# Expert weights in 2 MB transfers, with each expert's units in the order gate, gate, up, up, down, down

## The chip, the core and the metric

The kernel runs on one core of a Trainium2 chip. The metric is the time in microseconds of one execution on the device. Three executions of the kernel before took 1879.18, 1884.72 and 1877.73 us; their median, 1879.18 us, is what the changed kernel is compared with.

The engines are named as in the profile: PE multiplies matrices, and PEld is its loading of weights; DVE does elementwise work, ACT activation functions and copies, POOL indices and gathers, and SP issues most of the DMAs. Engines run on their own and wait for each other on semaphores.

## What is computed

The program is one step of a small two-layer decoder. Layer 0 ends in a dense SwiGLU. Layer 1 ends in a mixture of eight experts, of which each token uses two:

```python
def swiglu(x, w_gu, w_down):
    F = w_down.shape[-2]
    gu = x @ w_gu
    return (jax.nn.silu(gu[..., :F]) * gu[..., F:]) @ w_down

def moe_swiglu(x, w_router, w_gu, w_down):
    logits = jnp.einsum('btd,de->bte', x, w_router).astype(jnp.float32)
    top_val, top_idx = lax.top_k(logits, TOP_K)
    gates = jax.nn.softmax(top_val, axis=-1)
    ...
    for e in range(N_EXP):
        y = y + combine[..., e:e + 1] * swiglu(x, w_gu[e], w_down[e])
    return y
```

There are 264 tokens of width 1024; each expert has `w_gu` of 1024 x 7168 (gate columns first, then up columns) and `w_down` of 3584 x 1024, all in float32. The change concerns the experts alone.

## The kernel before

**Units.** An expert's weights are 42 units of 1 MB (128 partitions x 2048 numbers). The 3584 hidden columns are cut into NG = 7 groups `c` of 512. A group has two gate units and two up units (the upper and the lower 512 rows of `w_gu`, 512 columns) and two down units (256 rows of `w_down`). `ORDER` (L243, made by `unit_order`, L230) is the order of the units in a group: gate 0, up 0, gate 1, up 1, and then the two down units of group c-1. So the first group of an expert has four units, the next six have six, and two down units end the expert.

**The path of a unit.** SP fetches it into one of six buffers of 1 MB (`halves`, by `EXPERT_HALVES`), one DMA a unit (`load_unit`, the DMA is on L556). ACT copies it, rounded, into the first half of one of three split buffers (`unit_hi`, L982), and DVE writes the rounding error into the second half (`unit_lo`, a subtraction on L1091). PE then does 12 matmuls of 512 columns for it: four blocks of rows, three products of high and low parts each (`three`, L1654). In this text "hi" and "lo" are those two halves of a split.

**What waits for what.** SP waits to fetch unit u until unit u-6 has been split by DVE (semaphore `unit_split`). ACT waits for the landing of the unit and until PE has used unit u-3 (`units_used`), so at most three units stand split. PE waits for `unit_split`.

**Other work in a group.** After the second gate unit ACT computes the silu (L1040) before it splits the unit three places later; DVE multiplies it with the up product ("the hidden product", the multiplication on `sb` that L1091 shows) after the second up unit. After the next group's gate 1, PE transposes the hidden product (L1651); ACT and DVE split that (L1012 and L1091 on `split_he`) for the down units. These steps stand in each engine's program at fixed places of `ORDER`, three units behind PE.

**Between experts.** ACT scales the expert's rows (L1030); POOL adds them to a table in DRAM with an indirect DMA (L765, the scatter) and then gathers the rows of a later expert with another (L746, the gather). These use the same 16 DMA engines as the weights. ACT reloads its function table before the first split of an expert and again before its first silu.

The expert loop runs seven times, and the eighth expert is written out behind it. Of the first expert, six units are fetched early, during the mixer of layer 1.

Of the kernel before, what the change touches and what calls it, by code (L numbers as in the profile page):

```python
# [27 lines left out]
P = 128  # L28
D = 1024
KT = D // P  # L30
# [19 lines left out]
FF = 3584  # L50
FC = 512
NG = FF // FC
NE = 8
# [7 lines left out]
HALVES = 2 * SLOTS  # L61
UNITS = 6 * NG
SPLITS = 3
# [177 lines left out]


ORDER = unit_order()  # L243

LN_PARTS = {(0, 0): 0, (0, 1): KT // 2, "v": KT, (1, 0): KT + GB // 2}

# [5 lines left out]
def hybrid_step(nc, a, out):  # L252
# [4 lines left out]
    with ExitStack() as ctx:  # L257
# [270 lines left out]
        @block.sync  # L528
        def _(sp):
            def mixer_slabs(lay):  # L530
                for what, (n, slot, count, before) in slab_of.items():
                    if what[1] != lay:
                        continue
                    if before is not None:
                        sp.wait_ge(slabs_used, before + 1)
                    elif lay:

                        sp.wait_ge(sig("unit_split"), UNITS - HALVES + 2 * [1, 2, 0].index(slot) + 2)
                    src, k, cols = w_in_source(what)
                    sp.dma_start(as_slab(ring[slot], k, cols), src).then_inc(landed[slot], 16)  # L540

            def last_use(lay, slot):
                return max(n for what, (n, sl, _, _) in slab_of.items() if what[1] == lay and sl == slot) + 1

            def load_unit(u, w_gu, w_down, half, by_rows):

                kind, c, i = ORDER[u]
                w, c0, rows, cols = (w_down, 0, FC, D) if kind == "down" else (w_gu, c * FC + (FF if kind == "up" else 0), D, FC)
                if kind == "down":
                    w = w[c * FC:(c + 1) * FC]  # L550
                if by_rows:
                    w = w[i * rows // 2:(i + 1) * rows // 2, c0:c0 + cols]
                else:
                    w = w[:, c0 + i * cols // 2:c0 + (i + 1) * cols // 2]
                k = UNIT // (cols if by_rows else cols // 2)
                sp.dma_start(as_slab(halves[half], k, UNIT // k), w.rearrange("(k p) n -> p k n", p=P)).then_inc(half_landed[half], 16)  # L556

            sp.dma_start(xrows[:, 0:TT, :], a["x_prompt"][0].rearrange("(t p) d -> p t d", p=P)).then_inc(sig("x_landed"), 16)
            sp.dma_start(xrows[0:NS, TT, :], a["x_sample"].rearrange("b t d -> (b t) d")).then_inc(sig("x_landed"), 16)
            sp.dma_start(memrows[0], a["mem_prompt"][0].rearrange("(t p) d -> p t d", p=P)).then_inc(sig("mem0_landed"), 16)  # L560
            mixer_slabs(0)
            for u in range(UNITS):
                half = DENSE_HALVES[u % HALVES]
                if u >= HALVES:
                    sp.wait_ge(sig("unit_split"), u - HALVES + 1)
                else:
                    sp.wait_ge(slabs_used, last_use(0, half // 2))
                load_unit(u, a["ffn_w_gu"][0], a["ffn_w_down"][0], half, False)
            mixer_slabs(1)

            def expert_unit(e, t, u):
                if t is not None:

                    sp.wait_ge(sig("unit_split"), t * UNITS + (UNITS + u - HALVES + 1))
                load_unit(u, a["moe_w_gu"][0][bass.ds(e, 1)][0], a["moe_w_down"][0][bass.ds(e, 1)][0], EXPERT_HALVES[u % HALVES], True)


            for u in range(HALVES):
                sp.wait_ge(slabs_used, last_use(1, EXPERT_HALVES[u] // 2))
                expert_unit(0, None, u)  # L580
            with sp.Fori(0, NE - 1) as e:
                for u in range(HALVES, UNITS):
                    expert_unit(e, e, u)
                for u in range(HALVES):
                    expert_unit(e + 1, e + 1, u)
            for u in range(HALVES, UNITS):
                expert_unit(NE - 1, NE - 1, u)

            sp.wait_ge(sig("y_scattered"), 16 * NE)
            for tt in range(3):  # L590
                n = P if tt < TT else NS
                sp.dma_start(acc[0:n, tt, :], acc_dram[tt * P:tt * P + n, :]).then_inc(sig(f"acc{tt}_landed"), 16)
            sp.wait_ge(sig("routed"), 1)
            runs = sp.value_load(turn[0:1, 2 * NE:2 * NE + 1], min_val=NE, max_val=3 * NE)
            with sp.If(runs > NE):
                for chunk in (1, 2):
                    with sp.Fori(0, NE) as e:
                        n_tok = sp.value_load(counts[0:1, bass.ds(e, 1)], min_val=0, max_val=NT)
                        t = sp.value_load(turn[0:1, bass.ds(e + (chunk - 1) * NE, 1)], min_val=NE, max_val=3 * NE)
                        with sp.If(n_tok > chunk * P):  # L600
                            for u in range(UNITS):
                                expert_unit(e, t, u)
            sp.wait_ge(sig("y_out"), 16 * 3)

            for s in range(DEPTH):
                sp.wait_ge(sig(f"cache_out{s}"), 32)
            sp.wait_ge(sig("state_out"), 16)
            sp.wait_ge(sig("pstate_out"), 16)
            sp.wait_ge(sig("conv_out"), 48)
            sp.wait_ge(sig("sgu_out"), 16)  # L610
# [161 lines left out]
        def _(act):  # L772
# [203 lines left out]
            def unit_hi(t, u):  # L976

                if t is not None:
                    act.wait_ge(sig("units_used"), t * UNITS + (UNITS + u - SPLITS + 1))
                half = EXPERT_HALVES[u % HALVES]  # L980
                act.wait_ge(half_landed[half], (0 if t is None else t * 16 * NG) + 16 * (NG + u // HALVES + 1))
                act.activation(split_w[:, u % SPLITS, 0, :], halves[half], ACT.Copy).then_inc(sig("unit_hi"), 1)  # L982

            act.wait_ge(sig("attn1_lent_back"), 1)
# [47 lines left out]
            def expert(t, following):  # L1032

                for u in range(SPLITS, UNITS):
                    kind, c, i = ORDER[u - SPLITS]
                    if (kind, i) == ("gate", 1):
                        act.wait_ge(sig("units_used"), t * UNITS + (UNITS + u - SPLITS + 1))

                        act.wait_ge(sig("h_ready"), t * NG + (c - 2 + NG + 1))
                        act.activation(hsil[:, c % 2, :], ps[:, c % 2, :], ACT.Silu).then_inc(sig("silu_ready"), 1)  # L1040
                        if c:
                            hidden_T(t, c - 1)
                    if u == UNITS - 1:
                        if following:
                            gathered_hi(t + 1)
                        hidden_T(t, NG - 1)
                    unit_hi(t, u)
# [39 lines left out]
        def _(dve):  # L1087
# [479 lines left out]

            def expert(t, following, direct):
                for u in range(SPLITS, UNITS):
                    kind, c, i = ORDER[u - SPLITS]  # L1570
                    if (kind, i) == ("gate", 1) and c:
                        hidden_T(t, c - 1)
                    if (kind, i) == ("up", 1):
                        dve.wait_ge(sig("silu_ready"), t * NG + (c + 1))
                        dve.wait_ge(sig("units_used"), t * UNITS + (UNITS + u - SPLITS + 1))

                        if c >= 2:
                            dve.wait_ge(sig("T_done"), t * NG + (c - 1))
                        tt_(hgu[:, c % 2, :], hsil[:, c % 2, :], ps[:, 2 + c % 2, :], ALU.mult).then_inc(sig("h_ready"), 1)
                    if u == UNITS - 1:  # L1580
                        if following:
                            gathered_lo(t + 1)
                        hidden_T(t, NG - 1)
                    unit_lo(t, u)
                    if u == 4 and not direct:
                        selection_T(t)
# [52 lines left out]
        def _(pe):  # L1639
# [510 lines left out]
            def expert(t, following, direct):  # L2150

                pe.wait_ge(sig("xe_split"), t * 2 + 2)
                for u, (kind, c, i) in enumerate(ORDER):
                    if not direct:
                        if u == 2:
                            selection_T(t)
                        if u == 4:

                            pe.wait_ge(sig("selT_ready"), t * 2 + 2)
                            pe.wait_ge(sig("summed"), t * 3 + 4)  # L2160
                        if u == ORDER.index(("down", 0, 0)):

                            pe.wait_ge(sig("summed"), t * 3 + 6)
                    elif u == ORDER.index(("down", 0, 0)):

                        pe.wait_ge(sig("y_evicted"), t + 1)
                    if (kind, c, i) == ("down", NG - 2, 0) and following:
# [74 lines left out]
```

## Time and profile before

| | |
|---|---|
| median of three runs | 1879.18 us (1877.73 to 1884.72) |
| the profiled execution | 1885.63 us, its span 1883.9 us |
| PE busy | 1750.4 us, 93% of the span |
| DVE busy | 1239.7 us, 66% |
| ACT busy | 966.4 us, 51% |
| bytes read from HBM | 451.88 MB |
| the expert stage | from about 895 us to 1854 us |

The shares are means over unlike stages. Over the expert stage alone PE is busy nearly all the time and the DMA engines are too, so the stage has to be read by itself: what each engine waited for there, how long a fetch takes from issue to landing, and how much time lies between a landing and the use. PE's ends are modelled, and a busy PE is not proof of PE at its peak.

### The profile page before, as it was taken

The page shows a single profiled execution, that of the slowest core. Times are in us where ns is not written, and L with a number is a line of the kernel's source. Part 1 is how long each engine was busy: PE and PEld are TensorE (multiplying, and loading weights), DVE is VectorE, ACT ScalarE, POOL GpSimd, SP SyncE. Part 2 cuts the span into 40 slices and gives each one's busy share as a digit, 9 for nine tenths or more (in the row PEclk, how much of TensorE's full clock was granted, in tenths as well). Part 3 has the DMA queues.
Part 4 walks back from the last instruction along what each step waited for, and adds up shares of the span by engine and source line. Part 5 has one row for each costly group of instructions (what it writes and reads, how often), then busy time and mean ns, then how long its engine had stood idle before and what let it go on. Part 6 is the DMA issues. An engine that isn't in the chain of part 4 may idle for free.

```text
span 1883.9 us, 23515 instructions
## 1 busy us (share of the span) xinstructions
PE 1750.4 (93%) x8930; PEld 1470.7 (78%) x8931; DVE 1239.7 (66%) x1127; ACT 966.4 (51%) x846; POOL 124.8 (7%) x115
## 2 busy tenths in 40 slices
PE   7999799669999989796999999999999999999993
PEld 6867778559999958676887887888878888788882
DVE  2461345445666512235788888888888888888885
ACT  1342012143333222303777777787777777877772
POOL 4000152000000000002000001000010000000000
PEclk8997688889999989776999999999999999999997
DMA  7533002145555335015899999999999999999992
GB/s 261 197 134 103 1 0 68 35 158 189 181 183 182 135 129 176 7 47 201 286 372 360 395 377 364 383 365 394 371 369 382 363 388 380 364 385 366 381 381 75
DMA packets 212565, 465.55 MB, mean 247 GB/s; under 512 B 7368, under 2 KB 38243, under 8 KB 212451
## 3 DMA queue, kind: packets, MB, share of 16 engines
q1 hardware_dynamic: 203792, 433.20, 63.2%
q0 software_dynamic: 7568, 28.09, 5.1%
q10 hardware_dynamic: 1134, 3.29, 0.5%
q8 instruction: 47, 0.77, 0.2%
q14 instruction: 24, 0.20, 0.0%
HBM read 451.88 MB, written 12.82 MB: 247 GB/s over the span
## 4 chain that ended last, share of the span: by engine, by line
PE 73%; DVE 4%; ACT 3%; issue 1%; DMA 0%; ACTq 0%; DVEq 0%
PE ps L1654 70%; PE ps L1651 2%; DVE sb L1091 1%; DVE split_w L1091 1%; ACT split_w L982 1%; DVE sb L1337 1%; ACT sb L926 0%; PE ps L1802 0%; ACT L982 0%; ACT sb L1030 0%; DMA acc_rows<-sb,idx_to 0%; DVE sb L1362 0%; DVE sb L1624 0%; ACT sb L850 0%; DMA sb<-acc_rows 0%
## 5 line engine op out<-in xcount | busy, mean ns | idle before, releaser
L1091 DVE TENSOR_TENSOR split_w<-half_slots,split_w 128x2048 fp32r<-128x2048 f32 x378 | 860.7, 2289 | 208.3 <-ACT split_w L982 127.6
L982 ACT ACTIVATE split_w<-half_slots 128x2048 fp32r<-128x2048 f32 x336 | 643.4, 1919 | 222.1 <-PE ps L1654 169.7
L1654 PE MATMUL ps<-split_w,split_xe 128*128 128x512 f32 x2688 | 637.5, 393 | 4.6 <-DVE split_w L1091 2.9
L1654 PEld LDWEIGHTS ps<-split_w,split_xe 128*128 128x128 f32 x2688 | 500.4, 188 | 114.8 <-DVE split_w L1091 10.4
L1654 PE MATMUL ps<-sb 128*128 128x264 f32 (+11 forms) x2180 | 470.3, 378 | 51.3 <-DVEq L1339 10.5
L1654 PEld LDWEIGHTS ps<-sb 128*128 128x128 f32 (+4 forms) x2180 | 382.0, 220 | 136.7 <-issue 52.6
L1654 PE MATMUL ps<-split_w,split_he 128*128 128x512 f32 x1344 | 317.7, 391 | 0.0
L1654 PEld LDWEIGHTS ps<-split_w,split_he 128*128 128x128 f32 x1344 | 250.6, 188 | 54.4 <-issue 2.9
L1654 PE MATMUL ps<-x_hi,split_w 128*128 128x264 f32 x896 | 164.9, 286 | 13.4 <-DVE split_w L1091 13.4
L1654 PEld LDWEIGHTS ps<-x_hi,split_w 128*128 128x128 f32 x896 | 140.2, 191 | 13.8 <-DVE split_w L1091 13.8
L949 ACT ACTIVATE split_w<-half_slots 128x2048 fp32r<-128x2048 f32 x42 | 80.2, 1913 | 94.0 <-PE ps L1654 94.0
L1654 PE MATMUL ps<-x_lo,split_w 128*128 128x264 f32 x448 | 127.8, 285 | 0.0
L1091 DVE TENSOR_TENSOR sb<-sb,ps 128x384 f32<-128x384 f32 (+2 forms) x172 | 94.4, 567 | 46.0 <-PE ps L1654 41.7
L1651 PE MATMUL ps<-sb 128*128 128x128 f32 (+5 forms) x590 | 93.1, 299 | 30.4 <-DVEq L1191 7.0
L1651 PEld LDWEIGHTS ps<-sb 128*128 128x128 f32 (+5 forms) x590 | 76.5, 154 | 51.9 <-issue 20.4
L1654 PEld LDWEIGHTS ps<-x_lo,split_w 128*128 128x128 f32 x448 | 85.0, 190 | 0.0
L1654 PE MATMUL ps<-split_h,split_w 128*128 128x264 f32 x672 | 83.2, 285 | 0.0
L1654 PEld LDWEIGHTS ps<-split_h,split_w 128*128 128x128 f32 x672 | 82.7, 188 | 0.0
L765 POOL DMA_INDIRECT acc_rows<-sb,idx_to x8 | 18.8, 2351 | 875.7 <-ACT sb L1030 875.7
L1040 ACT ACTIVATE sb<-ps 128x512 f32<-128x512 f32 x56 | 33.6, 600 | 43.2 <-PE ps L1654 43.1
L1091 DVE TENSOR_TENSOR sb<-sb 128x264 f32<-128x264 f32 (+11 forms) x78 | 49.6, 649 | 2.8
L895 ACT ACTIVATE sb<-ps 128x384 f32<-128x384 f32 x24 | 11.6, 491 | 71.7 <-PE ps L1654 51.9
(208 smaller groups left out, 625.2 us busy)
## 6 DMA issues: line engine op xcount, KB each, us to landing
half_slots<-in_moe_w_gu SPq DMA_DIRECT2D x224, 1024.0 KB, 7.7
half_slots<-in_moe_w_down SPq DMA_DIRECT2D x112, 1024.0 KB, 7.5
half_slots<-in_ffn_w_gu SPq DMA_DIRECT2D x28, 1024.0 KB, 5.1
half_slots<-in_ffn_w_down SPq DMA_DIRECT2D x14, 1024.0 KB, 5.0
sb<-in_a_w_in SPq DMA_DIRECT2D x6, 2048.0 KB, 15.8
sb<-in_w_out SPq DMA_DIRECT2D x4, 2048.0 KB, 8.4
sb<-in_b_w_in SPq DMA_DIRECT2D x3, 2048.0 KB, 8.0
sb<-in_cache_mem_v POOLq DMA_DIRECT2D x2, 2048.0 KB, 19.0
```

The lines of the kernel that those rows point to most:

```text
L765: pool.indirect_dma_start(acc_dram, bass.IndirectOffsetOnAxis(ap=idx_to[:, e:e + 1], axis=0), yrows, None, compute_op=ALU.add).then_inc(si ...
L895: free(act.activation(pair(Y, i), src, ACT.Copy), "Y", n, s, i)
L949: act.activation(split_w[:, u % SPLITS, 0, :], halves[half], ACT.Copy).then_inc(sig("unit_hi"), 1)
L982: act.activation(split_w[:, u % SPLITS, 0, :], halves[half], ACT.Copy).then_inc(sig("unit_hi"), 1)
L1040: act.activation(hsil[:, c % 2, :], ps[:, c % 2, :], ACT.Silu).then_inc(sig("silu_ready"), 1)
L1091: return dve.tensor_tensor(o, x0, x1, op)
L1337: step(dve.reciprocal(sq[:, part, :], sq[:, part, :]))
L1651: return pe.transpose(o, i, ident[0:n, 0:n])
L1654: return pe.matmul(o, l, r, start=start, stop=stop)
```

## The change

Each pair of units of the same kind is fetched by one DMA of 2 MB into two neighbouring buffers. The order of units within an expert becomes gate, gate, up, up, down, down, so that the units of a pair follow each other. Of 336 fetches 168 are left. SP waits for the split of the later of the two units that last held the pair of buffers, and ACT waits, for either unit of a pair, for the landing of the whole pair. The dense layer keeps the old order and the old fetches.

```diff
+def expert_order():
+    order = []
+    for c in range(NG + 1):
+        if c < NG:
+            order += [("gate", c, 0), ("gate", c, 1), ("up", c, 0), ("up", c, 1)]
+        if c:
+            order += [("down", c - 1, 0), ("down", c - 1, 1)]
+    return order
+EXPERT_ORDER = expert_order()
...
-            def expert_unit(e, t, u):
+            def expert_units(e, t, u):
                 if t is not None:
-                    sp.wait_ge(sig("unit_split"), t * UNITS + (UNITS + u - HALVES + 1))
-                load_unit(u, a["moe_w_gu"][0][bass.ds(e, 1)][0], a["moe_w_down"][0][bass.ds(e, 1)][0], EXPERT_HALVES[u % HALVES], True)
+                    sp.wait_ge(sig("unit_split"), t * UNITS + (UNITS + u + 1 - HALVES + 1))
+                kind, c, _ = EXPERT_ORDER[u]
+                half = EXPERT_HALVES[u % HALVES]
+                if kind == "down":
+                    w, k = a["moe_w_down"][0][bass.ds(e, 1)][0][c * FC:(c + 1) * FC], FC // P
+                else:
+                    c0 = c * FC + (FF if kind == "up" else 0)
+                    w, k = a["moe_w_gu"][0][bass.ds(e, 1)][0][:, c0:c0 + FC], KT
+                into = half_slots[:, half:half + 2, :].rearrange("p h (k n) -> p (h k) n", k=k // 2)
+                sp.dma_start(into, w.rearrange("(k p) n -> p k n", p=P)).then_inc(half_landed[half], 16)
...
             with sp.Fori(0, NE - 1) as e:
-                for u in range(HALVES, UNITS):
-                    expert_unit(e, e, u)
+                for u in range(HALVES, UNITS, 2):
+                    expert_units(e, e, u)
...
                 half = EXPERT_HALVES[u % HALVES]
-                act.wait_ge(half_landed[half], (0 if t is None else t * 16 * NG) + 16 * (NG + u // HALVES + 1))
+                act.wait_ge(half_landed[half - half % 2], (0 if t is None else t * 16 * NG) + 16 * (NG + u // HALVES + 1))
...
                 for u in range(SPLITS, UNITS):
-                    kind, c, i = ORDER[u - SPLITS]
+                    kind, c, i = EXPERT_ORDER[u - SPLITS]
```

The last replacement is made in the programs of ACT and DVE; PE's loop runs over `EXPERT_ORDER` as well.

Three places show what moves. The first is SP's program at the head of the expert loop; `half_slots` are the six buffers, and `128x4x512` is 1 MB. Before:

```order
L556 ISA [waits unit_split]
L556 DMA half_slots<-in_moe_w_gu 128x4x512
L574 REGISTER_ALU
L556 ISA [waits unit_split]
L556 DMA half_slots<-in_moe_w_gu 128x4x512
L574 REGISTER_ALU
L556 ISA [waits unit_split]
L556 DMA half_slots<-in_moe_w_down 128x2x1024
```

And now:

```order
L599 ISA [waits unit_split]
L599 DMA half_slots<-in_moe_w_gu 128x8x512
L590 REGISTER_ALU
L599 ISA [waits unit_split]
L599 DMA half_slots<-in_moe_w_down 128x4x1024
```

Two waits and two DMAs of 1 MB have become one wait and one DMA of 2 MB.

The second is ACT's program at the start of an expert: the splits are on `split_w<-half_slots`, the silu is `sb<-ps 128x512`, each with a table load ahead of its first. Before:

```order
L982 ACT_TABLE_LOAD
L982 ACTIVATE split_w<-half_slots 128x2048
L979 REGISTER_ALU
L982 ACTIVATE split_w<-half_slots 128x2048
L1037 REGISTER_ALU
L1039 ISA
L1040 ACT_TABLE_LOAD
L1040 ACTIVATE sb<-ps 128x512
L982 ACTIVATE split_w<-half_slots 128x2048
```

And now:

```order
L1005 ACT_TABLE_LOAD
L1005 ACTIVATE split_w<-half_slots 128x2048
L1060 REGISTER_ALU
L1062 ISA
L1063 ACT_TABLE_LOAD
L1063 ACTIVATE sb<-ps 128x512
L1005 ACTIVATE split_w<-half_slots 128x2048
```

The first silu of an expert and its table load now stand behind one split (of unit 3) instead of two (of units 3 and 4).

The third is PE's program in the expert behind the loop, where rows are merged: `split_xe` marks gate and up units, 12 matmuls each, `split_he` down units, and `128x128 x4` the transposes of the hidden product. Before:

```order
L1654 MATMUL ps<-split_w,split_xe 128x512 x84
L1651 MATMUL ps<-sb 128x128 x4
L1654 MATMUL ps<-split_w,split_xe 128x512 x12
L1654 MATMUL ps<-split_w,split_he 128x512 x24
L1654 MATMUL ps<-split_w,split_xe 128x512 x36
```

And now:

```order
L1677 MATMUL ps<-split_w,split_xe 128x512 x72
L1674 MATMUL ps<-sb 128x128 x4
L1677 MATMUL ps<-split_w,split_xe 128x512 x24
L1677 MATMUL ps<-split_w,split_he 128x512 x24
L1677 MATMUL ps<-split_w,split_xe 128x512 x24
```

Between the transposes and the down units that need them there are now two units instead of one.

## Rows read from the trace of the kernel before

**Rows 1.** Stages: stretch, us, PE busy (instructions), granted clock, DMA share, GB/s.
```profile
1120.00:1240.00 120.00, 119.59 (x542) 1.00 1.02 375
```
**Rows 2.** Groups by line, 880 to 1884 us: count | busy, mean ns | idle before.
```profile
L1654 PE MATMUL ps<-split_w,split_xe 128*128 128x512 f32 x2688 | 637.5, 393 | 4.6 <-DVE split_w L1091 2.9 <-DVE split_xe L1091 1.6
```
**Rows 3.** Waits, 930 to 1884 us: who for whom, total us, times, longest.
```profile
ACT split_w L982 <- PE ps L1654: 166.1, 242, 1.1
```
**Rows 4.** Timeline of one group inside an expert: start us, length us, what.
```profile
1302.02 8.32 PE L1654 MATMUL ps<-split_w,split_xe 128*128 128x512 f32 x36
1310.54 3.00 PE L1654 MATMUL ps<-split_w,split_xe 128*128 128x512 f32 x12
1313.38 5.60 PE L1654 MATMUL ps<-split_w,split_he 128*128 128x512 f32 x24
1318.82 8.33 PE L1654 MATMUL ps<-split_w,split_xe 128*128 128x512 f32 x36
...
1310.46 0.60 ACT L1040 ACTIVATE sb<-ps 128x512 f32<-128x512 f32 x1 [0.88 <-PE ps L1654]
1311.43 1.92 ACT L982 ACTIVATE split_w<-half_slots 128x2048 fp32r<-128x2048 f32 x1
1313.58 1.92 ACT L982 ACTIVATE split_w<-half_slots 128x2048 fp32r<-128x2048 f32 x1 [0.22 <-PE ps L1654]
...
1313.39 2.29 DVE L1091 TENSOR_TENSOR split_w<-half_slots,split_w 128x2048 fp32r<-128x2048 f32 x1 [0.88 <-ACT split_w L982]
1316.19 4.49 DVE L1091 TENSOR_TENSOR split_w<-half_slots,split_w 128x2048 fp32r<-128x2048 f32 x2
...
1318.64 7.88 SPq L556 DMA_DIRECT2D half_slots<-in_moe_w_gu  x4
```
**Rows 5.** Timeline at the start of an expert, ACT and then PE.
```profile
1260.84 3.72 ACT L982 ACTIVATE split_w<-half_slots 128x2048 fp32r<-128x2048 f32 x2
1264.83 1.28 ACT L1040 ACT_TABLE_LOAD   x1 [0.28 <-PE ps L1654]
1266.62 3.71 ACT L982 ACTIVATE split_w<-half_slots 128x2048 fp32r<-128x2048 f32 x2
...
1265.13 11.61 PE L1654 MATMUL ps<-split_w,split_xe 128*128 128x512 f32 x48 [0.41 <-DVE split_w L1091]
1276.93 3.00 PE L1654 MATMUL ps<-split_w,split_xe 128*128 128x512 f32 x12
```
**Rows 6.** DMA issues by line: count, KB each, median us from issue to landing.
```profile
half_slots<-in_moe_w_gu SPq DMA_DIRECT2D x224, 1024.0 KB, 7.7
sb<-in_w_out SPq DMA_DIRECT2D x4, 2048.0 KB, 8.4
sb<-in_b_w_in SPq DMA_DIRECT2D x3, 2048.0 KB, 8.0
sb<-in_w_mem_kv SPq DMA_DIRECT2D x2, 2048.0 KB, 9.5
```
**Rows 7.** Landings of weight fetches issued at 900-1000, 1246-1260, 1260-1296, 1366-1380, 1380-1416, 1140-1176 us.
```profile
DMA to landing us min/median/max: 4.9/7.3/7.9
DMA to landing us min/median/max: 5.9/6.2/6.7
DMA to landing us min/median/max: 6.8/7.5/8.3
DMA to landing us min/median/max: 6.0/6.4/7.3
DMA to landing us min/median/max: 8.5/9.2/10.2
DMA to landing us min/median/max: 9.5/10.2/11.2
```
**Rows 8.** Timeline ahead of the first expert, ACT.
```profile
836.55 1.91 ACT L982 ACTIVATE split_w<-half_slots 128x2048 fp32r<-128x2048 f32 x1 [36.33 <-DMA half_slots<-in_moe_w_gu]
848.54 2.48 ACT L921 ACTIVATE sb<-sb 128x528 f32<-128x528 f32 x4 [10.08 <-DVE sb L1356]
```

More of the change, by code:

```diff
@@ L569, in _ @@
             mixer_slabs(1)
-            def expert_unit(e, t, u):
+            def expert_units(e, t, u):
                 if t is not None:
-                    sp.wait_ge(sig("unit_split"), t * UNITS + (UNITS + u - HALVES + 1))
-                load_unit(u, a["moe_w_gu"][0][bass.ds(e, 1)][0], a["moe_w_down"][0][bass.ds(e, 1)][0], EXPERT_HALVES[u % HALVES], True)
-            for u in range(HALVES):
+                    sp.wait_ge(sig("unit_split"), t * UNITS + (UNITS + u + 1 - HALVES + 1))
[8 more added lines that the diff above has]
+                sp.dma_start(into, w.rearrange("(k p) n -> p k n", p=P)).then_inc(half_landed[half], 16)
+            for u in range(0, HALVES, 2):
                 sp.wait_ge(slabs_used, last_use(1, EXPERT_HALVES[u] // 2))
-                expert_unit(0, None, u)
+                expert_units(0, None, u)
             with sp.Fori(0, NE - 1) as e:
-                for u in range(HALVES, UNITS):
-                    expert_unit(e, e, u)
[L584 to L587, printed above, removed]
+                for u in range(HALVES, UNITS, 2):
+                    expert_units(e, e, u)
+                for u in range(0, HALVES, 2):
+                    expert_units(e + 1, e + 1, u)
+            for u in range(HALVES, UNITS, 2):
+                expert_units(NE - 1, NE - 1, u)
             sp.wait_ge(sig("y_scattered"), 16 * NE)
@@ L600, in _ @@
                         with sp.If(n_tok > chunk * P):
-                            for u in range(UNITS):
-                                expert_unit(e, t, u)
+                            for u in range(0, UNITS, 2):
+                                expert_units(e, t, u)
             sp.wait_ge(sig("y_out"), 16 * 3)
@@ L1569, in expert @@
                 for u in range(SPLITS, UNITS):
-                    kind, c, i = ORDER[u - SPLITS]
+                    kind, c, i = EXPERT_ORDER[u - SPLITS]
                     if (kind, i) == ("gate", 1) and c:
@@ L2152, in expert @@
                 pe.wait_ge(sig("xe_split"), t * 2 + 2)
-                for u, (kind, c, i) in enumerate(ORDER):
+                for u, (kind, c, i) in enumerate(EXPERT_ORDER):
                     if not direct:
@@ L2160, in expert @@
                             pe.wait_ge(sig("summed"), t * 3 + 4)
-                        if u == ORDER.index(("down", 0, 0)):
+                        if u == EXPERT_ORDER.index(("down", 0, 0)):
                             pe.wait_ge(sig("summed"), t * 3 + 6)
-                    elif u == ORDER.index(("down", 0, 0)):
+                    elif u == EXPERT_ORDER.index(("down", 0, 0)):
                         pe.wait_ge(sig("y_evicted"), t + 1)
```

## The prediction

> **What bounds the kernel now.** I read the stages first. In the expert stage, taken over 120 us, the length of one expert, PE is busy 119.59 us at the full clock, and at the same time the DMA engines are busy all the time (share 1.02) at 375 GB/s [rows 1]. So two things are near a limit at once, and the question is which one leaves no room. The groups by line say it is PE: over all 2688 gate and up matmuls it sat idle only 4.6 us, nearly all of it for the split by DVE [rows 2]. The waits agree: ACT stood 166.1 us in 242 waits for PE to give back a split buffer, at most 1.1 us at a time, and among the waits no one stands for a landing of weights in this stretch [rows 3]. Weights land before they are wanted.
>
> The timeline gives the pace. Gate and up matmuls start at 1302.02 and again at 1318.82, so a group takes 16.8 us [rows 4]. Without the transposes (about 0.4 us) a unit takes PE (16.8 - 0.4) / 6 = 2.73 us. The split of a unit takes 1.92 us on ACT and then 2.29 us on DVE. With three split buffers ACT may begin when PE has two units left, 5.5 us, and 4.2 us are spent: there is some 1.2 us to spare, less where the silu comes in between. The stage therefore runs at PE's pace with two thin margins, that of the splitting and that of the fetching. The change touches both and takes nothing off PE: the same matmuls, the same splits. What it can gain is bounded by PE's waits.
>
> **The order of units inside an expert: about nothing.** I lay the new order on the durations of one group, with time 0 at the start of the silu, 1310.46 [rows 4]. Before, PE starts the second up unit at 0.08, the down units at 2.92 and 5.64, the next gate at 8.36; ACT splits the second down unit from 0.97 and DVE ends it at 2.93 + 2.29 = 5.22, 0.42 before PE wants it. Now the silu stands behind the second gate, and PE goes on with up 0 at 0.08, up 1 at 2.92, down at 5.64 and 8.36, the next gates at 11.08 and 13.81, up 0 (behind the transposes) at 16.9. The split behind the silu is now that of the first down unit, done at the same 5.22 and wanted at the same 5.64. DVE then splits down 1 (to 7.51), does the hidden product (the two splits around it stand 0.5 apart, 1313.39 + 2.29 against 1316.19), and splits gate 0 (8.0 to 10.3, wanted at 11.08) and gate 1 (10.5 to 12.8, wanted at 13.81). Nothing is late. The hidden rows' own split, which had one unit of PE's time to hide under, now has two.
>
> **The order at the start of an expert: +5 us.** Here ACT has no time to spare. Before, it splits units 3 and 4 from 1260.84 to 1264.56, then loads the table and does the silu, and starts on unit 5 at 1266.62: 2.06 us for the two. PE takes unit 3 at 1265.13 [rows 5]. The change puts these 2.06 us ahead of unit 4. Unit 3's split ends on ACT at 1262.76; unit 4's then runs to 1262.76 + 2.06 + 1.92 = 1266.74 there and to 1269.07 on DVE. PE would want it at 1265.13 + 2.73 = 1267.86: late by 1.2 us. Part comes back, since waits for the units after it vanish. Unit 5 is ready at 1271.36 and wanted at 1271.80, unit 6 follows the transposes at 1274.89, unit 7 comes at 1277.7, against 1276.93 before [rows 5]: 0.75 us a time. Seven experts of eight pay it (the expert behind the loop has no table load), 7 x 0.75 = 5.2, and I take 5. Its bounds are 3 (if the chip overlaps more) and 8.4 (1.2 us each, nothing comes back).
>
> **The fetches: +5 us, between 0 and 20.** Each packet stays a row of 2 or 4 KB, so bandwidth is the same. What shrinks is the room between issue and need. A pair may be fetched only when its second unit has been split, and must have landed whole when ACT wants the first. On the timetable above the gate pair's buffers come free at 12.8, and ACT wants the next gate pair when PE has done with up 1 (5.8, next group 22.6): 9.8 us. For the up pair it is also 9.8, for the down pair (7.5 to 0.97 + 16.8) 10.3. SP needs 0.16 to issue (split done at 1316.19 + 2.29, issue at 1318.64) [rows 4]. That leaves 9.7 to 10.1. A late landing is first paid from the spare of the splits (0.4 for down, about 1 for gate, 1.3 for up), so PE begins to stop at landings of about 10.5 us after the issue. Before, the same reckoning for single units gives 2.73 more.
>
> How long does a pair take? The least that 1 MB took is 4.9 us [rows 7], the median 7.7; transfers of 2 MB in the mixers took 8.0, 8.4 and 9.5 [rows 6]. Where the queue is backed up the pair's last byte is asked for when that of the second unit was before, so it lands when that did. I take 8.2 in quiet stretches. That leaves 10.5 - 8.2 = 2.3 us of room, where single units had 10.5 + 2.7 - 7.7 = 5.5. Then there are the bursts: seven times, when a finished expert is scattered and a later one gathered, landings climb. From a median of 6.2 to a worst of 8.3 in the mildest case, from 6.4 to 10.2 in the sharpest; the worst of all is 11.2 [rows 7]. So a burst adds 2.1 to 3.8 us, 2.9 at the middle, on 8.2: 11.1, over the 10.5 by 0.6, seven times 4 us, and 1 us for smaller bumps elsewhere. That is 5. If pairs land as singles did in the burst, only the few over 10.5 pay (11.2 and its like), 1 us in all. If quiet pairs take 9.5 like the slowest row, a burst ends at 12.4 and costs 1.9, 13 in all, and smaller bumps pay too: 20.
>
> The Trainium skill (DMA: Bandwidth & Descriptors, Anatomy of one DMA) puts one DMA at about 2.0 us plus its bytes over 436 GB/s; an estimate for 2 MB from it is 6.8 us. By that the room would be 3.7 and this term nil. The mixers' rows of 8.0 to 9.5 disagree.
>
> **Ahead of the experts: nothing.** The first pairs land some 3 us later than a first single unit. ACT waits 36.33 us for one landing and splits at 836.55, to 838.46; its next work is at 848.54 [rows 8]. Ten microseconds cover the 3. If that cover were gone, the norm behind it would pay the 3 once.
>
> **Sum.** 5 + 5 = 10 us. On the profiled execution that is 1885.63 + 10 = 1895.6; that execution was 6.45 us over the median of the runs, so I forecast 1879.2 + 10 = 1889 us. A measurement of this kernel can tell about 0.5% (9.4 us) from no change; the forecast lies just beyond.
>
> **The rivals.**
> - *The fetches hide after all.* The bursts may be taken up by the splits' spare and by time that PE lost at the expert's start. Then only the order costs, 1884 us. For it: bursts come right at the start of an expert, where PE is late anyway. Against it: 8.2 + 2.9 is over 10.5. The other side of my forecast is here: within 0.5%.
> - *Fetches become the bound.* If pairs take 9.5 in quiet stretches, ACT waits for landings in many groups, and the time is 1879 + 5 + 17 = 1901, up to 1906. It decides from a quiet landing of about 9.3. For it: the DMA engines have no idle time [rows 1]. Against: 1 MB lands in 5 to 6 us when nothing disturbs it [rows 7].
> - *Faster.* Half the fetches and half the waits on them could let DMA run ahead, and PE's waits vanish. The skill's rule on the same page (Bandwidth: batch to 1 MiB or more, with efficiency still rising at 16 MB) points this way. But all that PE waits for is 4.6 us [rows 2], and it waits for splits, not landings: at the best 1875, within 0.5%; beyond would need faster matmuls.
>
> **How the numbers follow.** Forecast (1885 to 1895): 0.50, of it 0.32 beyond 0.5%. Fetches hidden, 1884 (1880 to 1888): 0.28. Fetches bound, 1901 (1896 to 1906): 0.18. Faster, 1875 or less: 0.04, of it 0.02 beyond 0.5%. Slower is 0.32 + 0.18 = 0.50, same 0.18 + 0.28 + 0.02 = 0.48, faster 0.02. The range is 1880 to 1906: all but the gain and the far end of the bursts.
>
> **What would show it.** In the profile after: no change before 895 us. At each expert's start PE waits over 1 us for DVE's split of unit 4, seven times. 2 MB fetches land at a median of 8 to 9 us. ACT's waits name a landing of weights, which they don't now, in a cluster behind each scatter and hardly elsewhere. If no such waits show, the second term is wrong; if they show all through the experts, the third rival is right. If PE's group takes other than 16.8 us in quiet stretches, my timetable of the order is wrong. A granted clock below full in the stage would make all of it wrong.

## The result and the profile after

The changed kernel took 1898.64 us (median of 7 runs, 1893.34 to 1901.15), the kernel before 1883.57 us on the same chip (7 runs, 1877.73 to 1885.77). The ratio is 1.0084 with an interval of 1.0065 to 1.0103: slower by some 16 us, between 12 and 19. The profiled execution took 1900.83 us, its span 1899.1.

The chain that ended last, by engine, on the page of the kernel before:

```profile
PE 73%; DVE 4%; ACT 3%; issue 1%; DMA 0%; ACTq 0%; DVEq 0%
```

The page of the kernel after: the same chain, the group of the gate and up matmuls (busy, mean ns | idle time before), and the fetches (count, KB, median us to landing).

```profile
PE 59%; DMA 9%; DVE 6%; ACT 5%; issue 2%; ACTq 0%; DVEq 0%; SPq 0%
...
L1677 PE MATMUL ps<-split_w,split_xe 128*128 128x512 f32 x2688 | 640.1, 394 | 19.8 <-DVE split_w L1114 18.1
...
half_slots<-in_moe_w_gu SPq DMA_DIRECT2D x112, 2048.0 KB, 9.8
half_slots<-in_moe_w_down SPq DMA_DIRECT2D x56, 2048.0 KB, 9.4
```

In the chain, DMA has 9% of the span, 0% before. The second row answers [rows 2]: in front of the gate and up matmuls PE sat idle 19.8 us, 4.6 before. A fetch of 2 MB took 9.8 and 9.4 us at the median, against 7.7 for 1 MB [rows 6].

The stretch of [rows 1] again (us, PE busy, ..., granted clock, DMA share, GB/s):

```profile
1120.00:1240.00 120.00, 118.36 (x537) 97.03 (x536) 103.80 (x57) 90.68 (x62) 3.58 (x2) 1.00 1.01 372
```

The clock is full, as before, and the DMA share too. The rate has not risen from 375 GB/s but fallen a little, with the pace; PE is busy 1.2 us less.

The waits between 930 and 1884 us, kernel after (who for whom, total us, times, longest):

```profile
ACT split_w L1005 <- PE ps L1677: 104.3, 165, 3.5
ACT split_w L1005 <- DMA half_slots<-in_moe_w_gu: 79.5, 47, 4.9
...
PE ps L1677 <- DVE split_w L1114: 17.7, 23, 2.3
...
ACT split_w L1005 <- DMA half_slots<-in_moe_w_down: 11.9, 11, 1.8
```

In [rows 3] ACT waited 166.1 us for PE and never for a landing. Now 91.4 us of its waits, in 58 places, are for landings, and what it waited for PE has shrunk to 104.3. PE in turn waits for splits that come late.

**How long the expert stage takes.** The row of a tile gives the first and the last start of its matmuls. The stage begins with the first matmul on `split_xe` and ends with the last on `split_he`. Kernel before, then after:

```profile
L1654 PE MATMUL ps<-split_w,split_xe x2688: 387/389/791, 894.9 to 1842.3; 128*128 128x512 f32 x192
L1654 PE MATMUL ps<-split_w,split_he x1344: 387/389/493, 919.9 to 1853.8; 128*128 128x512 f32 x192
```

```profile
L1677 PE MATMUL ps<-split_w,split_xe x2688: 387/389/787, 889.3 to 1857.6; 128*128 128x512 f32 x192
L1677 PE MATMUL ps<-split_w,split_he x1344: 387/389/497, 914.8 to 1869.0; 128*128 128x512 f32 x192
```

From 894.9 to 1853.8 and the 0.4 of the last matmul, 959.3 us; after, from 889.3 to 1869.0, 980.1: 20.8 us more. The profiled executions are only 15.2 us apart (1900.83 - 1885.63), since the part ahead of the experts was 5.6 us shorter in this one. Over the traces of all kernels below, whose programs up to there differ only in how the first fetches are grouped, the stage begins anywhere from 886.3 to 894.9. I compare stages therefore, and give the ratio of the times beside them. A stage is one execution: where landings are late it may itself differ by some us, and the profiled execution of the changed kernel is the second slowest of its seven. Over all runs the loss is nearer to 16 than to 20.8.

### The profile page after: what moved, and what is told of

The parts are those of the page before. It is cut to its first block, busy times and chain, and to the rows that moved or that the text cites. A ratio compares the mean times of both kernels' runs of the same rounds, so it can differ in the third digit from the quotient of the medians.

```text
span 1899.1 us, 22906 instructions
## 1 busy us (share of the span) xinstructions
PE 1747.1 (92%) x8930; PEld 1465.1 (77%) x8931; DVE 1239.6 (65%) x1127; ACT 965.3 (51%) x846; POOL 117.5 (6%) x115
## 4 chain that ended last, share of the span: by engine, by line
PE 59%; DMA 9%; DVE 6%; ACT 5%; issue 2%; ACTq 0%; DVEq 0%; SPq 0%
PE ps L1677 57%; DMA half_slots<-in_moe_w_gu 6%; DVE split_w L1114 3%; ACT split_w L1005 3%; DMA half_slots<-in_moe_w_down 2%; PE ps L1674 2%; DVE sb L1114 1%; DVE sb L1360 1%; ACT sb L949 0%; PE ps L1825 0%; DMA acc_rows<-sb,idx_to 0%; ACT L1063 0%; DVE sb L1385 0%; ACT L1005 0%; ACT sb L1053 0%
## 5 line engine op out<-in xcount | busy, mean ns | idle before, releaser
L1677 PE MATMUL ps<-split_w,split_xe 128*128 128x512 f32 x2688 | 640.1, 394 | 19.8 <-DVE split_w L1114 18.1
L1677 PE MATMUL ps<-sb 128*128 128x264 f32 (+11 forms) x2180 | 461.3, 372 | 50.2 <-DVEq L1362 10.5
L1677 PEld LDWEIGHTS ps<-sb 128*128 128x128 f32 (+4 forms) x2180 | 373.8, 215 | 135.3 <-issue 51.9
L1674 PE MATMUL ps<-sb 128*128 128x128 f32 (+5 forms) x590 | 94.9, 303 | 32.7 <-DVEq L1310 8.4
## 6 DMA issues: line engine op xcount, KB each, us to landing
sb<-in_cache_mem_v POOLq DMA_DIRECT2D x2, 2048.0 KB, 18.9
```

The lines of the kernel that those rows point to most:

```text
L1674: return pe.transpose(o, i, ident[0:n, 0:n])
L1677: return pe.matmul(o, l, r, start=start, stop=stop)
```

## The experiments

The change has three parts: the order; that a pair is asked for only when both its buffers are free (late issue); that neither unit may be split until both have landed (joint landing). The theory on record is that the order costs ACT time at an expert's start, and that pairs have too little room between issue and need in the bursts of scatter and gather. Its rivals are that pairs land late everywhere, so that fetches are the bound, and that the large DMA as such is the cost. Each time is compared with runs of the kernel before on the same chip; each stage is one trace.

| kernel | stage, us | against 959.3 | time against before |
|---|---|---|---|
| order alone, 1 MB fetches | 961.2 | +1.9 | 1.0004 [0.9991, 1.0016] |
| order, late issue | 961.3 | +2.0 | 1.0017 [1.0004, 1.0031] |
| order, joint landing | 961.5 | +2.2 | 1.0015 [0.9999, 1.0031] |
| order, late issue and joint landing, 1 MB | 974.9 | +15.6 | 1.0064 [1.0040, 1.0089] |
| the changed kernel (the same in 2 MB) | 980.1 | +20.8 | 1.0084 [1.0065, 1.0103] |
| old order, 2 MB | 992.0 | +32.7 | 1.0187 [1.0162, 1.0212] |
| old order, late issue and joint landing, 1 MB | 992.1 | +32.8 | 1.0144 [1.0094, 1.0194] |
| before, without scatters | 959.6 | +0.3 | one run |
| after, without scatters | 964.2 | +4.9 | one run |
| before, one table load less | 956.7 | -2.6 | 0.9982 [0.9971, 0.9994] |
| order alone, one table load less | 954.3 | -5.0 | 0.9984 [0.9973, 0.9995] |
| after, one table load less | 973.7 | +14.4 | 1.0069 [1.0049, 1.0088] |

**The order alone.** `EXPERT_ORDER` in all programs, with one 1 MB DMA a unit at its own time.

```diff
-                load_unit(u, a["moe_w_gu"][0][bass.ds(e, 1)][0], a["moe_w_down"][0][bass.ds(e, 1)][0], EXPERT_HALVES[u % HALVES], True)
+                kind, c, i = EXPERT_ORDER[u]
...
+                sp.dma_start(as_slab(halves[half], k, UNIT // k), w.rearrange("(k p) n -> p k n", p=P)).then_inc(half_landed[half], 16)
```

> The new order of units, but each unit of 1 MB fetched by itself as in the kernel before. Theory (most of the loss comes from the room between issue and need that pairing takes): only the start of an expert pays, 2 to 5 us in the expert stage (959.4 us before, 980.1 us with the whole change, from the first expert matmul to the last), ratio 1.001 to 1.003, no wait of ACT for a landing of weights. Rival (the order itself is what costs): 15 to 20 us, ratio 1.008.

The time can't be told from before, and the 1.9 us of stage lie just under the 2 to 5 expected. No wait for a landing shows in the stage. The timeline of this kernel at an expert's start, PE and then ACT, to be read beside [rows 5]:

```profile
1254.64 8.32 PE L1674 MATMUL ps<-split_w,split_xe 128*128 128x512 f32 x36
1263.37 3.04 PE L1674 MATMUL ps<-split_w,split_xe 128*128 128x512 f32 x12 [0.41 <-DVE split_w L1111]
1267.08 5.78 PE L1674 MATMUL ps<-split_w,split_xe 128*128 128x512 f32 x24 [0.68 <-DVE split_w L1111]
...
1278.61 5.60 PE L1674 MATMUL ps<-split_w,split_he 128*128 128x512 f32 x24
...
1295.42 2.88 PE L1674 MATMUL ps<-split_w,split_he 128*128 128x512 f32 x12
```

```profile
1259.07 1.92 ACT L1002 ACTIVATE split_w<-half_slots 128x2048 fp32r<-128x2048 f32 x1
1261.01 1.28 ACT L1060 ACT_TABLE_LOAD   x1
...
1262.80 5.64 ACT L1002 ACTIVATE split_w<-half_slots 128x2048 fp32r<-128x2048 f32 x3
```

Unit 3 starts at 1263.37 and unit 4 at 1267.08, 3.71 later, where 2.73 is a unit's time: PE is late by 0.98, and I had worked out 1.2. The silu's table load stands at 1261.01 behind one split, as the order of the program said. Of the delay more comes back than I thought. The first down unit starts 23.97 us behind the expert's first matmul (1278.61 - 1254.64), before the change 23.37 (1279.77 - 1256.40): 0.60 late. At the end of the expert only 0.3 of it is left: from the second expert on, the first matmuls of two experts are 120.24 to 120.29 us apart, before 119.95 to 119.97.

**Late issue, joint landing, and both.** All three in the new order and in 1 MB DMAs. Late issue: both DMAs of a pair are issued when the later buffer is free. Joint landing: each DMA at its own time, and ACT waits for both landings. The third does both, and differs from the changed kernel only in that a pair is two DMAs.

```diff
+                if t is not None:
+                    sp.wait_ge(sig("unit_split"), t * UNITS + (UNITS + u + 1 - HALVES + 1))
+                for v in (u, u + 1):
...
+                if u % 2 == 0:
+                    act.wait_ge(half_landed[half + 1], (0 if t is None else t * 16 * NG) + 16 * (NG + u // HALVES + 1))
```

The upper piece is late issue, the lower one joint landing.

> As the run with two DMAs of 1 MB issued together, but ACT waits for each unit's own landing. Theory (room): the first unit of a pair has its last byte 2.7 us sooner, so it gets back the 2.7 us and bursts are nearly covered: 4 to 8 us slower in the expert stage, of it 2 to 5 from the order. Rival (issuing late is enough to starve the DMA engines): 15 us or more.

> The new order, each unit fetched by its own DMA of 1 MB as soon as its own buffer is free, but ACT waits for the landing of both units of a pair before it takes the first. Theory (late issue and joint landing each take 2.7 us of room, and only both together use it up): 1.8 us from the order and 1 to 4 us from bursts alone, so 962 to 965 us in the expert stage against 959.4 before and 974.8 with both. Rival (waiting for the pair's landing is the whole cost, whenever it was asked for): 12 us or more.

> The whole change, but each pair fetched by two DMAs of 1 MB, issued one behind the other at the moment of the one of 2 MB; ACT waits for both landings before the first unit. Theory (room: it is when a pair is asked for and when it is wanted): as the change, 17 to 22 us slower in the expert stage. Rival (one DMA of 2 MB is itself slower than two of 1 MB): 2 to 6 us, as the order alone.

ACT's waits for landings, 930 to 1884 us: joint landing (for down units 0.4 us more), then both. With the late issue there is one such wait, of 1.2 us.

```profile
ACT split_w L1004 <- DMA half_slots<-in_moe_w_gu: 11.8, 9, 2.1
```

```profile
ACT split_w L1005 <- DMA half_slots<-in_moe_w_gu: 82.3, 44, 3.9
...
ACT split_w L1005 <- DMA half_slots<-in_moe_w_down: 7.0, 8, 1.8
```

Each alone adds 0.1 to 0.3 us to the stage over the order's 961.2; both together add 13.7. The waits show the same: 1.2, 12.2 and 89.3 us. That fits a room that each uses up in part and that both together exceed. Late issue alone cost less than I expected (4 to 8 us, of it 2 to 5 from the order; measured 2.0 in all), both together a little less than the 17 to 22 (15.6); joint landing alone, at 961.5, lies just under its 962 to 965. The size of the DMA isn't what costs most: with 1 MB DMAs, whose landings are at a median of 7.8 us, nearly three quarters of the loss are there (13.7 of 18.9). By the single landings of that trace, the second DMA of a pair lands 9.4 us behind the issue of the first, at the median, close to the 9.7 of the DMAs of 2 MB over the stage. Whether one DMA of 2 MB costs 5 us more than two of 1 MB stays open: 980.1 against 974.9 are one trace each, and the intervals of the times overlap.

**The pairs in the old order.** The same fetch of 2 MB without the new order (gate and up units of the same rows are then one DMA), and the same late issue and joint landing in 1 MB DMAs.

```diff
+                into = half_slots[:, half:half + 2, :]
...
+                    w = a["moe_w_gu"][0][bass.ds(e, 1)][0][i * D // 2:(i + 1) * D // 2]
+                    w = w.rearrange("(k p) (h f) -> p h k f", p=P, h=2)[:, :, :, c * FC:(c + 1) * FC]
+                    sp.dma_start(into.rearrange("p h (k n) -> p h k n", k=4), w).then_inc(half_landed[half], 16)
```

> The old order with fetches of 2 MB: one DMA takes a gate unit and the up unit behind it (same 512 rows, two ranges of columns), the down units go in pairs. Theory (room): 14 to 18 us slower in the expert stage, ratio 1.007 to 1.010, ACT waits for landings some 90 us in all. Rival (the order costs): within 3 us of before.

> The old order, pairs as units stand in it (gate with up, down with down), each pair fetched by two DMAs of 1 MB issued together, both landings waited for. Theory (in the old order a down pair has only 8.6 us from its issue to its need, against 10.1 in the new one, and that is why the fetch of 2 MB cost more there): 20 to 33 us slower in the expert stage, with some 40 waits for w_down, 50 us or more. Rival (the 2 MB DMA over two ranges of columns was slow by its shape): 12 to 16 us, as in the new order, and few waits for w_down.

The loss is 33 us of stage in either form, over half as much again as with the new order; by the times it is 1.9% and 1.4%, and the profiled execution with 1 MB DMAs is the slowest of its four. For the fetch of 2 MB I had expected 14 to 18 us and some 90 us of waits: a miss, from which the second run followed, and that came out as expected. The waits say where, first for 2 MB, then for two DMAs of 1 MB:

```profile
ACT split_w L989 <- DMA half_slots<-in_moe_w_gu: 83.8, 59, 4.1
...
ACT split_w L989 <- DMA half_slots<-in_moe_w_down: 60.7, 40, 3.0
```

```profile
ACT split_w L983 <- DMA half_slots<-in_moe_w_gu: 68.8, 47, 3.8
ACT split_w L983 <- DMA half_slots<-in_moe_w_down: 54.9, 32, 3.7
```

Waits for down units have gone from 11.9 to 55 to 61 us. The timelines show their room: in the old order (two DMAs of 1 MB) from the issue of a down pair to the split of its first unit, and then the same for the changed kernel.

```profile
1328.49 0.93 SPq L556 DMA_DIRECT2D half_slots<-in_moe_w_down  x2
...
1337.06 1.92 ACT L983 ACTIVATE split_w<-half_slots 128x2048 fp32r<-128x2048 f32 x1 [0.80 <-PE ps L1655]
```

```profile
1074.72 0.37 SPq L599 DMA_DIRECT2D half_slots<-in_moe_w_down  x1
...
1085.14 3.85 ACT L1005 ACTIVATE split_w<-half_slots 128x2048 fp32r<-128x2048 f32 x2
```

8.6 us in the old order, 10.4 in the new one. The new order puts the silu and the hidden rows' split ahead of the first down unit on ACT instead of between the two. So the order isn't the cost of this change; with it, pairs cost less than without it. That the 1.8 us of room are the reason rests on these two places and on the waits for down units.

**Without the scatters.** In both kernels a finished expert's rows are not added to the table, and the rows of the first expert stand for those of all later ones; weights, splits and matmuls are as they were.

```diff
-                    fetch(e + 1)
...
-                pool.indirect_dma_start(acc_dram, bass.IndirectOffsetOnAxis(ap=idx_to[:, e:e + 1], axis=0), yrows, None,
-                                        compute_op=ALU.add).then_inc(sig("y_scattered"), 16)
+                pool.sem_inc(sig("y_passed"), 1)
```

> The kernel before without the scatter of each expert's rows and without the gathers behind the first (every expert works on the first one's rows; the sums in DRAM stay without the experts). Theory: PE sets the pace, so the expert stage stays within 1 us of 959.4; landings behind each expert's start no longer climb over 8.5 us.

> The changed kernel without scatters and without the gathers behind the first. Theory (the loss is bursts on too little room): 964 to 968 us in the expert stage against 980.1 with them, with ACT's waits for landings down from 91 us to under 30. Rival (a pair takes too long even in quiet stretches): 974 us or more, waits stay over 60 us.

Landings in the expert stage (889 to 1855 us) of before and of after, each as it is and then without scatters:

```profile
DMA to landing us min/median/max: 4.9/7.7/11.2
```

```profile
DMA to landing us min/median/max: 4.8/7.2/8.3
```

```profile
DMA to landing us min/median/max: 7.7/9.7/14.5
```

```profile
DMA to landing us min/median/max: 7.7/9.4/11.1
```

The scatters and gathers make the worst landing, 14.5 against 11.1 us, and hardly the median: pairs land at 9.4 us without any scatter. Single units don't feel the scatters (959.6 against 959.3). Pairs do: 980.1 against 964.2, so in these traces some 16 of the 20.8 us come with the scatters. Each of the two kernels without scatters ran once. What I expected of the waits was wrong: ACT still waited 57.2 us in 45 places for landings, where I had less than 30. These waits are short, 2.2 us at most, and cost PE little: it waits 6.9 us for splits, where it waited 17.7 with scatters and 6.6 with the order alone. The waits of the changed kernel without scatters:

```profile
ACT split_w L1002 <- DMA half_slots<-in_moe_w_gu: 52.2, 40, 2.2
...
PE ps L1674 <- DVE split_w L1111: 6.9, 14, 0.7
```

**One table load less.** To take away the late silu without undoing the order, ACT does a silu of one column at the head of each expert, into a column nobody reads. It was put into all three kernels.

```diff
             def expert(t, following):
+                act.activation(rstd[:, 0:1], eps_ln, ACT.Silu)
```

> The new order with single 1 MB fetches, and one more instruction: ACT does a silu of one column, into a spare column that nobody reads, as the first thing in the loop of an expert, while PE still works through the first three units. Then the function table of the silu should be in place when the first real silu comes, and the load of 1.28 us ahead of it goes. If the table load is what makes unit 4 late in the new order, PE's wait for the split of unit 4 (0.99 us in seven experts) is gone and those of unit 3 too (0.57, since the load ahead of the first split is then earlier): the eight experts take 957 us instead of 961.2, 4 us less, and a ratio to the kernel before of 0.998 to 0.999. If the silu's own time and the wait for the gate product set it, the stage stays at 960 to 961. If copies need a table of their own, there are now two loads behind each other, the first split comes 1.3 us later, and the stage is 962 or longer.

> The changed kernel with the same one-column silu at the head of each expert. If its loss is in the fetches and not in ACT's late splits, the stage stays at 977 to 980 us, the time within 0.2% of the changed kernel's (ratio to the kernel before 1.006 to 1.0085), and ACT's waits for landings stay at 85 to 95 us. If late splits at the start of an expert push the whole chain (a late split makes a late issue, which lands late in the burst), the gain is more than the 2 to 4 us of the table load: the stage falls to 970 or less, the ratio to 1.004 or less.

> The kernel before with the same one-column silu at the head of each expert. PE waits there about 0.57 us before unit 3 and 0.5 us in all before the units behind it, in seven experts. If the table loads make these, up to 1.1 x 7 = 8 us could go, and I expect half, 3 to 4 us: stage 955.5 us, ratio 0.998. If the rows' own splits make the wait before unit 3, it is 957 to 959, ratio 0.999 to 1.0.

ACT at the start of an expert in the kernel with the order alone:

```profile
1250.48 1.28 ACT L1054 ACT_TABLE_LOAD   x1
1251.78 0.20 ACT L1054 ACTIVATE sb<-sb 128x1 f32<-128x1 f32 x1
1251.89 1.90 ACT L1002 ACTIVATE split_w<-half_slots 128x2048 fp32r<-128x2048 f32 x1
1253.70 0.57 ACT L1061 ACTIVATE sb<-ps 128x512 f32<-128x512 f32 x1
1254.17 3.71 ACT L1002 ACTIVATE split_w<-half_slots 128x2048 fp32r<-128x2048 f32 x2
```

One table load of 1.28 us stands there, none ahead of the real silu at 1253.70, and PE no longer stops ahead of unit 4; ahead of unit 3 it still stops 0.5 us. With the order the stage is 6.9 us shorter, more than the 4 expected, and 2.4 us shorter than the old order with the same edit; by the times the two are the same. The changed kernel gains 6.4 us of stage, which lies between what the two theories gave. The old order gains 2.6, less than the 3 to 4 expected. But its waits for landings are what they were (92.8 us, 91.4 without the edit) and its loss against its own counterpart is 19.4 us, against 18.9. Late splits on ACT are therefore not what makes the pairs late. The two kernels with single fetches and this edit are the fastest of all, by 0.2%.

## Why the prediction was right in direction and short in size

**What bounds the kernel.** Right. PE's pace, and the two margins beside it, one of which gave way.

**Order inside an expert, nothing.** Right. In the rows above, 1278.61 to 1295.42 is a group of 16.81 us.

**Order at an expert's start, +5.** Its mechanism is there, seven times, but the term was too large: 1.9 us by the stage, 0.8 by the times, under my lower bound of 3. I let 0.45 of 1.2 come back; measured are 0.98 and 0.3 that stay.

**Fetches, +5 between 0 and 20.** This is the step that failed: 18.9 us by the stage (980.1 - 961.2), 15 by the times (0.8% of 1880). Its parts one by one. The room was right. Here is a group of the kernel after, far from any scatter (PE, ACT, SP):

```profile
1072.79 5.60 PE L1677 MATMUL ps<-split_w,split_he 128*128 128x512 f32 x24
...
1080.11 5.81 SPq L599 DMA_DIRECT2D half_slots<-in_moe_w_gu  x2
...
1089.58 5.61 PE L1677 MATMUL ps<-split_w,split_he 128*128 128x512 f32 x24
1090.52 3.92 ACT L1005 ACTIVATE split_w<-half_slots 128x2048 fp32r<-128x2048 f32 x2 [1.53 <-DMA half_slots<-in_moe_w_gu]
...
1095.03 5.61 PE L1677 MATMUL ps<-split_w,split_xe 128*128 128x512 f32 x24
```

The gate pair issued at 1080.11 (the first of two in that row) has landed when ACT goes on at 1090.52, 10.4 us later, and ACT has stood 1.53 for it. PE goes on without a stop: the down units start 16.79 us apart, and the next gate units at 1095.03. A landing of 10.4 is thus free, as the 10.5 of the prediction has it.

What I mis-sized is the landing of a pair that no scatter disturbs. I had 8.2, and the pair above took 10.4. Landings of pairs in the kernel after, issued at 1160 to 1230 and at 1290 to 1376 (both away from an expert's start), then at 1008 to 1030 (an expert's start):

```profile
DMA to landing us min/median/max: 7.8/8.3/10.4
DMA to landing us min/median/max: 8.4/10.0/11.2
DMA to landing us min/median/max: 10.7/13.6/14.5
```

And at the start of the same expert in the changed kernel without scatters, issued at 1012 to 1034:

```profile
DMA to landing us min/median/max: 9.9/10.6/10.8
```

Some quiet stretches have the 8.2, others 10. Without any scatter the median of the whole stage is 9.4 and the worst 11.1. So of the 2.3 us of room only 1.1 is left before the burst comes. The height of the burst I had nearly right: from 10.6 to 13.6 at the median of this start, 3.0 us, and from 11.1 to 14.5 at the worst of the stage, 3.4; I had 2.9, between 2.1 and 3.8, and the worst landings of single units above, 8.3 and 11.2, give 2.9. My own other case, quiet pairs of 9.5 us, a burst that ends at 12.4 and 13 to 20 us in all, is the one that came. The sign I had given, that 2 MB fetches land at a median of 8 to 9 us, was missed too: they take 9.4 to 9.8.

The 8.2 was chosen from transfers in the mixers, whose medians hide how far apart they are. Of the three 2 MB transfers of `in_b_w_in`, median 8.0, two were issued at 631 and 642 us and one at 689:

```profile
DMA to landing us min/median/max: 7.7/7.8/8.0
DMA to landing us min/median/max: 13.3/13.3/13.3
```

From 631 to 652 us the DMA share was 0.58, from 689 to 703 it was 0.93, and in the experts it is 1.02 [rows 1]. The page also has six 2 MB transfers of `in_a_w_in` at a median of 15.8 us, which the prediction left out. That it is the load of the DMA engines that makes pairs land later in the experts is likely by these rows, but no run shows it by itself.

The start of the expert at 1011.28 shows the price:

```profile
1008.18 5.40 SPq L599 DMA_DIRECT2D half_slots<-in_moe_w_gu  x2
...
1014.69 2.56 POOL L788 DMA_INDIRECT acc_rows<-sb,idx_to  x1 [122.92 <-ACT sb L1053]
...
1019.45 3.71 ACT L1005 ACTIVATE split_w<-half_slots 128x2048 fp32r<-128x2048 f32 x2
...
1027.69 3.71 ACT L1005 ACTIVATE split_w<-half_slots 128x2048 fp32r<-128x2048 f32 x2 [4.53 <-DMA half_slots<-in_moe_w_gu]
...
1031.98 7.36 PE L1677 MATMUL ps<-split_w,split_xe 128*128 128x512 f32 x24 [2.07 <-DVE split_w L1114]
```

The second fetch in the row of 1008.18, an up pair, is issued at 1013.21 (that row ends at 1013.58, an issue takes 0.37), and the scatter follows at 1014.69. ACT is free for the pair at 1023.16, 9.95 us behind the issue; I had reckoned with 9.7 to 10.1. It lands at 1027.69, after 14.5. ACT stands 4.53 us and PE 2.07. From this expert's first matmul to the next one's it takes 124.17 us, the longest of this kernel; the same expert took 119.96 before.

**Ahead of the experts, nothing.** Nothing shows: the stage begins at 889.3, inside the 886.3 to 894.9 of all traces.

**The sum and the rivals.** I forecast +10; it became some 16 (the medians are 15.1 apart), a sum of one term too large and one far too small. That they partly cancel is luck, and so is a part of the number's lying in the range. The measured 1898.64 lies outside the 1885 to 1895 of the forecast itself and inside the 1896 to 1906 of the rival that fetches become the bound; 4.4 us of the distance from 1889 are the kernel before, at 1883.57 over seven runs where I had 1879.18.

*Fetches hide* fell: 18.9 us of stage are theirs. *Fetches become the bound* was nearer than I allowed. Its condition came: it was to decide from a quiet landing of about 9.3, and without scatters the median is 9.4. Its sign came too: of the 58 waits of ACT for landings 40 end more than 30 us behind an expert's first matmul. Its price did not: without scatters, pairs cost the stage only 2.7 us beyond the order's 1.9. PE stops behind the scatters, as I had forecast. By the starts of its matmuls, the second to seventh expert take 2.5 us longer each than with the order alone, and 2.0 of that lie in the first eleven units. So the bursts are the place of the loss, and on landings of 9.4 in place of 8.2 each costs more than I had.

*Faster* fell: fewer and larger DMAs moved no byte sooner. The estimate of 6.8 us for 2 MB, which I worked out from the Trainium skill (DMA: Bandwidth & Descriptors, Anatomy of one DMA), is under every landing of a pair: the least is 7.7 us, with the DMA engines busy all the time. That section measures DMAs issued from GpSimd, and these are issued from SP.

Why a pair lands at 8 us in one stretch and at 10 in another, with no scatter near, isn't shown. That scatter and gather together bring most of the loss is shown, by one trace each with and without; how they share the engines with two outstanding pairs is not.

## What to carry to other kernels

When transfers are merged in a ring of buffers that stays the same size, lay out two times for each: from its issue (the later buffer is free) to the first use of any part, and from its issue to its landing beside the worst neighbour on the queues, and compare these, not medians. Late issue and joint landing were each nearly free here and together, with the order, cost 0.6% of the time; try each by itself. Take the quiet landing from the stage itself: 8.2 us, chosen from transfers of the same size in another stage, was 1.2 too kind, and that was half of the room.

## What the runs showed of the hardware that was not expected

- The scatter and gather behind an expert (POOL stands up to 9.6 us for the scatter to land before it gathers) cost single fetches nothing, 959.3 us of stage with and 959.6 without, and raised the worst landing of pairs from 11.1 to 14.5 us.
- Among traces whose programs ahead of the experts do the same work, that part took 886.3 to 894.9 us, while from the second expert on an expert's period repeats to 0.05 us where fetches are single (120.24 to 120.29 with the order alone). In these traces the spread of the times with single fetches lies ahead of the experts.
- A silu of one column at the head of an expert saved a table load of 1.28 us: with it in place, copies and silus followed each other with no further load (1250.48 to 1254.17 above).
